# The last quad's first down pieces: rows 0 to 15 as two transfers of eight rows

## The reference

```python
x = layernorm(DN_ALPHA * x + merged @ lp['w_out'], lp['ln1_g'], lp['ln1_b'])
moe_out = hier_moe(x, lp['w_rg'], lp['w_re'], lp['w1'], lp['w3'], lp['w2'])
ple_term = jax.nn.sigmoid(x @ lp['w_ple_gate']) * (ple @ lp['w_ple'])
x = layernorm(DN_ALPHA * x + moe_out + ple_term, lp['ln2_g'], lp['ln2_b'])
```

## Time and profile before

| | before |
|---|---|
| median of 3 runs | 1526.13 us (1526.11 to 1533.0) |
| profiled execution | 1530.24 us |
| its span | 1528.46 us |
| mean granted TensorE clock | 0.913 |
| TensorE busy | 1272.7 us, 83% |
| VectorE busy | 436.2 us, 29% |
| ScalarE busy | 284.1 us, 19% |
| bytes moved | 505.60 MB, mean 331 GB/s |
| chain that ended last | PE 55%, DMA 35%, DVE 4%, SP's queue 3% |

### The profile page before, as it was taken

The page is one execution under the profiler, slowest core; times in us unless marked ns, Lnnn a source line. Parts: engine busy times, 40 slices in busy tenths (PEclk is TensorE's granted clock), DMA queues, the critical chain, the costliest instruction groups (busy, mean ns, idle before and its releaser), DMA issues.

```text
span 1528.5 us, 21258 instructions
## 1 busy us (share of the span) xinstructions
PE 1272.7 (83%) x8912; PEld 739.2 (48%) x8913; DVE 436.2 (29%) x1101; ACT 284.1 (19%) x712; POOL 71.3 (5%) x110
## 2 busy tenths in 40 slices
PE   7999899999787767767799998999996787677665
PEld 4767897554332323322266678976352323223211
DVE  4242753542111101001143547445311111011003
ACT  3343422021001101000044434211111011010001
POOL 1301000000000000000022011000000000000000
PEclk9999999999898877778899999999998988778888
DMA  9505966989999999999972079669999999999994
GB/s 332 164 1 152 255 168 225 399 355 429 430 428 429 430 431 429 431 429 428 379 255 84 3 198 297 180 229 417 378 429 431 431 429 430 430 430 430 429 425 173
DMA packets 85330, 505.60 MB, mean 331 GB/s; under 512 B 7600, under 2 KB 13680, under 8 KB 54128
## 3 DMA queue, kind: packets, MB, share of 16 engines
q1 hardware_dynamic: 75392, 476.47, 75.9%
q0 software_dynamic: 9840, 27.71, 8.4%
HBM read 492.87 MB, written 2.89 MB: 324 GB/s over the span
## 4 chain that ended last, share of the span: by engine, by line
PE 55%; DMA 35%; DVE 4%; SPq 3%; ACT 1%; issue 1%; POOL 0%; DVEq 0%
PE bank L1109 53%; DMA ring<-in_w_e_up 7%; DMA ring<-in_w_e_down 5%; DMA ring<-in_w_e_gate 5%; DMA arena<-in_w_e_up 4%; DMA arena<-in_w_e_gate 4%; DMA cst<-in_w_e_down 4%; DMA cst<-in_w_e_gate 3%; DMA arena<-in_w_e_down 2%; PE bank L1159 2%; SPq L921 2%; DMA ring<-in_w_in 1%; SPq L982 0%; DVE cst L2333 0%; DVE arena L2337 0%
## 5 line engine op out<-in xcount | busy, mean ns | idle before, releaser
L1109 PE MATMUL bank<-arena 128*32 128x512 f32 (+11 forms) x2808 | 568.5, 537 | 175.7 <-DMA ring<-in_w_e_up 48.7
L1109 PE MATMUL bank<-ring,arena 128*32 128x512 f32 (+4 forms) x1360 | 416.9, 646 | 36.4 <-DMA arena<-in_w_e_gate 18.7
L1109 PEld LDWEIGHTS bank<-arena 128*32 128x32 f32 (+6 forms) x2808 | 208.5, 137 | 436.4 <-issue 423.7
L1109 PE MATMUL bank<-ring,xT 128*32 128x128 f32 (+5 forms) x1536 | 237.3, 364 | 1.3 <-ACT xT L1728 1.1
L1109 PEld LDWEIGHTS bank<-ring,xT 128*32 128x32 f32 (+1 forms) x1536 | 121.5, 137 | 100.7 <-issue 90.2
L1109 PEld LDWEIGHTS bank<-ring,arena 128*32 128x32 f32 (+1 forms) x1360 | 107.0, 130 | 126.7 <-issue 119.8
L1109 PE MATMUL bank<-xT,ring 128*128 128x144 f32 (+1 forms) x640 | 111.8, 335 | 0.0
L1109 PEld LDWEIGHTS bank<-xT,ring 128*128 128x128 f32 x640 | 96.2, 190 | 13.6
L1109 PE MATMUL bank<-arena,x_sb 128*128 128x128 f32 (+1 forms) x768 | 99.7, 282 | 1.4 <-DVE arena L2496 0.8
L1109 PEld LDWEIGHTS bank<-arena,x_sb 128*128 128x128 f32 (+1 forms) x768 | 90.5, 190 | 19.4 <-issue 12.7
L1109 PE MATMUL bank<-cst,arena 128*32 128x512 f32 x144 | 82.7, 728 | 0.0
(11 more groups left out here) (250 smaller groups left out, 1008.4 us busy)
## 6 DMA issues: line engine op xcount, KB each, us to landing
arena<-in_w_e_up SPq DMA_DIRECT2D x30, 2048.0 KB, 28.9
arena<-in_w_e_gate SPq DMA_DIRECT2D x28, 2048.0 KB, 27.7
ring<-in_w_e_gate SPq DMA_DIRECT2D x24, 2048.0 KB, 25.6
arena<-in_w_e_down SPq DMA_DIRECT2D x20, 2048.0 KB, 23.0
ring<-in_w_e_down SPq DMA_DIRECT2D x18, 2048.0 KB, 24.3
ring<-in_w_in SPq DMA_DIRECT2D x32, 1024.0 KB, 9.5
ring<-in_w_e_up SPq DMA_DIRECT2D x16, 2048.0 KB, 25.0
arena<-in_w_e_gate SPq DMA_DIRECT2D x16, 1024.0 KB, 14.4
```

Source lines behind the costliest of these rows:

```text
L1109: return pe.matmul(out, lhsT, rhs, start=first, stop=last, skip_group_check=True)
```

## The change

The first down pieces of the last quad (k = 184 to 187, in both layers) are no longer loaded by `load_expert` as one transfer of 128 rows. `load_by_rows` waits for the slot as before and then issues three transfers into it: rows 0 to 7, rows 8 to 15, and rows 16 to 127. Each adds 16 to the slot's semaphore, so the planned count of that fill is 3 where it was 1. A row is 8 KB. Nothing else is changed: order, slots, waits and matmuls stay.

```diff
+FIRST_ROWS = [(0, 8), (8, 16)]
+
+def in_rows(k):
+
+    return (QUADS * 6 - 2) * QUAD <= k < (QUADS * 6 - 1) * QUAD
...
-                count[i] += 2 if last[i] is not None and first_released(last[i]) else 1
+                count[i] += 2 if last[i] is not None and first_released(last[i]) else 1 + len(FIRST_ROWS) * in_rows(k)
...
+                def load_by_rows(k):
+
+                    g, i = divmod(k, len(MOE_PIECES))
+                    w, h, e = MOE_PIECES[i]
+                    n = layer * LAYER_PIECES + len(PIECES) + k
+                    await_slot(n)
+                    for a, b in FIRST_ROWS + [(FIRST_ROWS[-1][1], P)]:
+                        sp.dma_start(slot(n)[a:b, :], experts[w][g * QUAD + e, a:b, h, :]).then_inc(ring_full[SLOT_OF[n]], 16)
...
                     if in_units(k):
                         if k // QUAD % 2 == 0:
                             load_unit(k)
+                    elif in_rows(k):
+                        load_by_rows(k)
                     elif k not in ks:
                         load_expert(k)
```

## The result

The changed kernel takes 1552.9 us, median of 6 runs (1550.75 to 1556.57), against 1526.81 for the kernel before in the same session: ratio 1.0163, interval 1.0146 to 1.0181, or 24.9 us more. The forecast was no change. The profiled execution took 1553.31 us with a span of 1551.5, 23.0 us over the span of before.

The account below looks back on a forecast made before the run. Each layer was taken to end with its last weight's last byte; uneven engine loads gave plus 0.4 and minus 0.2 us, SP's issues and waits nothing, so 1526.13 + 0.2 = 1526.3 us, range 1523.4 to 1533.0.

Parts of the forecast that it names:

- What bounds the kernel: End of each layer: TensorE waits for the last weight's last byte; level queues would bring at most 3.0 us a layer.
- The last sign that I named: Forecast wrong altogether if the stretch before the tail, and not the tail, is what changes.
- Which engines carry the rows: First down pieces: 8-row transfers use 8 engines, one row each; minus to plus 1.22 us a layer, 0.2 us in all.
- the 1.22 us: Four 8 KB rows more on one half of the engines, four less on the other: plus or minus 1.22 us a layer.
- the price of a row: In the first down pieces, an 8 KB row takes one engine 0.306 us, from 428 GB/s for 16 engines.
- SP's queue: Eight more issues a layer; six delay the half pieces by 1.5 to 2.6 us, covered by full queues, so cost nothing.
- Rival C: Tail of each layer: eight extra SP issues take 2.12 us each, 4.1 us a layer, 1534.3 us; chance 0.06.
- The waits: TensorE waits for 48 where it was 16, no instruction more; at worst starts 0.1 us late, taken up by idle: nothing.
- Rival D: Each short transfer holds its engines 1.9 us, eight cost 15.2 us a layer: 1556.5 us; chance 0.03.
- The sign I named: In layer 1 before the tail, a DMA share under 0.95 between 1484 and 1500 would show Rival D.

Follow-up runs that it names:

- the kernel with own places: Against the kernel before: half of each first down piece, as eight 8-row transfers written four rows apart, each engine where a 128-row transfer puts its rows; ratio 0.9990.
- the deciding pair: Two kernels against the kernel before, same eight 8-row reads of half of each piece: written every fourth row, ratio 0.9990; written side by side, 1.0089.
- The last experiment: Against the kernel before: 8-row transfers written four rows apart, alternating lower and upper half, so eight engines each use their own and an idle engine's place; ratio 1.0064.

## Why the prediction was wrong, point by point

- **What bounds the kernel**: right. All of the loss is in the two stretches that end with the last byte of a layer, and it moves the end one for one, but for the 1.6 us a layer that the faster clock gives back. The last sign that I named came true: the stretch before the tail is what changed. The last 5 us are much as before: a share of 0.44 from 1525 to 1530, and 42.1% in the earlier trace rows.
- **Which engines carry the rows**: right in the count. An 8-row transfer runs on 8 engines with one row each, as the packets of the kernel with own places show. Which half the last queues belong to was not measured: the 1.22 us are lost in a term ten times as large.
- **The step that failed** is the price of a row: "At 428 GB/s for 16 engines one engine moves 26.75 KB in 1 us, so a row of 8 KB takes 0.306 us", and before it "The bytes stay the same". I counted how many rows each engine gets and never asked where they lie. In the 112-row transfers, to which I gave no cost of their own, 16 busy engines move 201 to 256 GB/s and not 424: a row takes about 0.6 us and not 0.306, and the stretch loses 12.6 us a layer. The price from the earlier trace rows was that of engines in their own places; there it holds for 8-row transfers too (0.32 us a row).
- **The evidence that misled** is the earlier trace rows: 429 GB/s while five short transfers pass. It speaks against a fixed time for a short transfer, and in that it was right. But those rows are 16 packets of 512 B and 32 smaller ones, next to nothing beside 1.29 MB; they could not show what 8 KB rows do when they lie across the others' places.
- **SP's queue**: right for the twelve issues themselves. Nine took 0.34 us each, forecast as 0.25 to 0.43, and the other three fell ahead of a wait. Wrong for the half pieces behind them, which were to be 2.6 us late at most: the last one is issued at 746.09 in layer 0, where it was 737.34, 8.8 us later, and 7.2 us later in layer 1 beyond what is carried over, because SP waits on queues that drain at half the rate. It still has 22 us to landing, in full queues. Rival C is refuted by the column cut, with as many issues, at a ratio of 1.0000.
- **The waits**: not put to a test by themselves.
- **Rival D** (0.03, 1556.5 us) came closest in time and is wrong in its mechanism: short transfers in their own places cost nothing (0.9990), and without any short transfer the 112 rows cost 20.2 us. A right number from a wrong cause.
- **The sign I named** would have failed: "A share under 0.95 between 1484 and 1500". The share stayed at 1.0 at half the rate, so it counts an engine that is held up in its packet as busy.

What is shown: with the same reads, the same engines and the same number of transfers, the rows' places in the on-chip memory alone make the difference between 0.9990 and 1.0089; and the same engines in the same two places are fast when the others rest and slow when they work. So engines slow each other down by where they write. The Trainium skill has the map: "DMA: Bandwidth & Descriptors", section "The descriptor swizzle", says that in a 128-row transfer each engine writes one port, engine 0 rows 0 to 3 and 32 to 35, engine 8 rows 64 to 67 and 96 to 99, and so on. The kernel that writes rows four apart follows that map, and it is the only cut by rows alone that lost nothing. By the Trainium skill, "SBUF — State Buffer", section "Door 1: The DMA port swizzle (why [64,N] ≈ [32,N])", the bandwidth depends on how many of 16 ports a transfer's rows reach; the section "Can I just issue two DMAs to hit both halves?" of that page says that only one transfer spanning all 128 rows reaches all. By its last part the change was a loss from the start, and I should have made it a rival. The cut into two halves agrees with the first part (8 ports; 241 GB/s, about half the rate). Its measure does not hold here: 16 rows seven apart reach 14 ports by its formula and gave 197 GB/s, 16 rows side by side reach 4 and gave 234. So in these full queues the number of ports of one transfer does not sort the runs. What does, in the runs with whole rows, is whether engines leave their own places while others write.

Open: why the loss comes out near half in nearly every cut, and how one engine's write holds up the others, also those whose place it does not touch (below). That the queues drift out of step and collide at random was only argued. The same reads were used in the deciding pair, so a part of the reads in the other runs isn't excluded.

## What to carry to other kernels

If a weight load like this one has to be cut, cut it by columns: three transfers with all 128 rows cost nothing here, and cuts of these pieces by rows that made engines write in each other's places cost 9.8 to 25.5 us; none was faster than leaving them whole. Read GB/s beside the DMA share, since a share of 1.0 at 220 GB/s is a stall that looks like work. And before a price per row is taken from a trace, ask whether the rows of that trace go where the new ones will go.

## What the runs showed of the hardware

A transfer whose engines leave their own places slows the 128-row transfers that drain beside it. The last experiment shows it, since its packets can be told apart by size: rows of 8 KB belong to the eight engines with the first down pieces, rows of 4 KB to half pieces. From 1496 to 1498:

```profile
DMA packets 149, 0.57 MB, mean 283 GB/s; under 512 B 45, under 2 KB 45, under 8 KB 115
...
q1 hardware_dynamic: 149, 0.57, 104.0%
```

There are 34 rows of 8 KB and 70 of 4 KB, 139 and 143 GB/s. The eight alone moved 205, and the other eight would move 211 at the rate of the earlier trace rows: both sets are slowed.

The loss is also not confined to the engines whose places are used by two. From 1500 to 1504 most of the eight have gone on to half pieces, in their own places:

```profile
DMA packets 309, 1.15 MB, mean 288 GB/s; under 512 B 47, under 2 KB 47, under 8 KB 290
...
q1 hardware_dynamic: 309, 1.15, 101.2%
```

Only 19 rows of 8 KB pass in these 4 us, which at 0.6 us each keep three engines busy at most. As an estimate, were each of the three to slow only the one engine whose place it uses, and all six to run at half the rate of the earlier trace rows, 26.4 GB/s an engine, the 16 would move 343 GB/s. They move 288, at a share of 1.01. So engines that write in their own places, and share them with nobody at that time, are slowed too; how, no run here shows.

The 20 matmuls behind a layer's last landing take 1.6 us less in the changed kernel. The granted clock is the cause that the rows show; first the changed kernel, then the one before.

```profile
1531.00:1535.00 4.00, 3.93 (x21) 1.39 (x22) 1.42 (x3) 0.59 (x1) 0.00 (x0) 1.00 0.00 0
```

```profile
1506.00:1512.00 6.00, 5.61 (x21) 1.83 (x22) 1.47 (x3) 0.58 (x1) 0.00 (x0) 0.72 0.00 0
```

The first of these matmuls in the changed kernel, with the idle time before it:

```profile
1531.07 0.62 PE L1128 MATMUL bank<-arena 128*32 128x512 f32 x1 [2.07 <-DMA arena<-in_w_e_down]
```

The clock is 1.00, the level of 2.4 GHz, after TensorE had been idle for 2.07 us, and a mean of 0.72 over both levels where it had been idle for 2.90 us; the 20 matmuls take 3.88 us in place of 5.50.
